# Splitting the summed weights one step earlier, and signalling the activation differences in two steps, in a fast-product feed-forward kernel

## The chip, the cores and the metric

One core of a Trainium2 chip runs the whole program. The metric is device time in microseconds (us) of one execution. Engines are named as the profile names them: PE is TensorE (its sequencer PEq), PEld its weight loads, DVE is VectorE, ACT is ScalarE, POOL is GpSimd, SP only issues transfers. Instructions of one engine run in program order; between engines there are only semaphores.

## The reference, cut to what matters

Two layers, each with two SwiGLU feed-forward sublayers ("FFN steps") around a mixer; all in float32, 640 tokens (512 sample, 128 prompt), model width 1024, inner width 2816:

```python
def _swiglu(h, wg, wu, wd):
    return (jax.nn.silu(h @ wg) * (h @ wu)) @ wd

def _layer(x, mod, p, tables, ctx_ckv, ctx_krope):
    ...
    h = _rmsnorm(x, p["norm_ffn1"]) * (1 + sc1) + sh1
    x = x + 0.5 * g1 * _swiglu(h, p["w_ffn1_gate"], p["w_ffn1_up"], p["w_ffn1_down"])
    ...
    x = x + g2 * m
    h = _rmsnorm(x, p["norm_ffn2"]) * (1 + sc3) + sh3
    x = x + 0.5 * g3 * _swiglu(h, p["w_ffn2_gate"], p["w_ffn2_up"], p["w_ffn2_down"])
    return x, ckv_n, krope
```

`mod` (the shifts sh, scales sc and gates g) comes from a small product of conditioning vectors with `w_mod`.

## The kernel before, in words

**Split products.** Every operand is held as a rounded part (`_hi`, made by ACT) and a remainder (`_lo`, made by DVE as whole minus rounded part, by the helper `lo_of`, L1830). A product is three matmuls: hi by hi (L731), hi weights by lo activations (L733), lo weights by hi activations (L735).

**Seven products for eight.** An FFN step has 22 pairs (one tile of 128 gate columns and one of 128 up columns). Gate and up, and the two halves of the model width, form a 2 by 2 block product, computed by seven products of half size, P1 to P7, each 4 tiles by 3 matmuls of 320 or 322 columns. They use sums of weight tiles, made by POOL in `weight_sums` in three additions (L695 for S1 and S3, L699 for S2, L702 for S4), and differences of activation halves. For pair g, weights are split in five pieces: `hi_11/lo_11` for P1, `hi_12/lo_12` for P2, `hi_22/lo_22` for P4, `hi_s/lo_s` (two summed tiles, 1024 columns) for P5 and P6, and `hi_34/lo_34` (the other two summed tiles, 1024 columns) for P3 and P7.

**The order of a cycle.** PE runs, for pair g: P2, P6, P5, P7, then P1 of pair g + 1, sometimes small products for `mod` (L785), then P4 and P3. PE waits for the `lo` piece of each. P3 of the pair g - 1 is thus the last product ahead of P2 of pair g. DVE combines the results from PSUM: `c11` (L2007), `u2` (L2012), `u2_p5` (L2018), `u3` (L2023), `c22` (L2028), `c21` (L2032), then the up half is scaled (`up_scaled`, L2038); `c12` (L2043) and `gate_scaled` (L2048) finish the gate of the pair one cycle later, `gated` (L2053) multiplies after ACT's `silu_of` (L1436) and `up_bias` (L1442), and `a_rest` makes `a_lo` after ACT's `a_part` (L1448). `ga` and `ub`, `prod` and `silu` are views of one buffer, so `c11` of a pair waits for `gated` of the one before.

**POOL.** The sums of pair g + 1 may start when both summed pieces of pair g are split (`s_los`, `s_lo34`), since `sums_raw` holds one pair. For the first pair of a chunk they wait for the down tiles instead.

**Chunks.** The 22 pairs are in four chunks of 5 or 6 (16 chunks in the program: eight of 6, eight of 5). After a chunk the eight down tiles are computed with `a_hi`, `a_lo` and added to `x` by DVE (L1969). For the first pair of a chunk the summed pieces are split during the down tiles.

**The start of an FFN step.** For k = 0 to 7, ACT scales a tile of x (`split_h`, L1411, L1414), DVE makes two steps of differences (L1844, L1833, L1850) and `h_lo`; after each odd k `split_differences(nn, i)` rounds three pieces on ACT (L1419 `t_hi` of 640 columns, L1420 `t_hi` and L1421 `h_hi` of 320) and takes three remainders on DVE (`t_lo` twice, `h_lo`). P6 of the first pair waits for each i (`s_tlo`). ACT's `copy_a1` (L1431), the first in a chain to `norm_rows` (L771: ACT `hi_11`, DVE `lo_11`, `c11`, `u2`, `lo_12`, `u2_p5`, `c12`, a reciprocal, ACT `diagonal` L1366), and POOL's sums of the second pair wait for all of them.

Of the kernel before, what the change touches and what calls it, by code (L numbers as in the profile page):

```python
# [267 lines left out]
def build(nc, i, o):  # L268
    ctx = ExitStack()
    with ctx:  # L270
# [386 lines left out]
        @block.gpsimd  # L657
        def _(pool):
            pool.sem_inc(s_split, CREDIT)
            pool.sem_inc(s_rot, START)  # L660
            nc.gpsimd.memset(ones[:], 1.0).then_inc(s_fill, 1)
            nc.gpsimd.memset(eps[:], EPS).then_inc(s_fill, 1)
            nc.gpsimd.memset(cond[:], 0.0).then_inc(s_fill, 1)
            nc.gpsimd.memset(ident[:], 0.0).then_inc(s_fill, 1)
            nc.gpsimd.memset(r_one[:, T:TB], 1.0).then_inc(s_fill, 1)
            pool.wait_ge(s_fill, 5)
            nc.gpsimd.affine_select(out=ident[:], in_=ident[:], compare_op=ALU.not_equal, fill=1.0, base=0,
                                    pattern=[[-1, P]], channel_multiplier=1).then_inc(s_fill, 1)
            nc.gpsimd.memset(group_ones[0][:, 0:1], 1.0).then_inc(s_fill, 1)

            def rotate(hd):

                pool.wait_ge(s_q32, hd + 1)
                nc.gpsimd.tensor_tensor(rot[NOPE:QK], q32[QK:P], rope_tab[QK:P, :], ALU.mult).then_inc(s_rot, 1)
                pool.wait_ge(s_rot, hd * 3 + 1 + START)
                nc.gpsimd.tensor_tensor(q32[NOPE:QK], q32[NOPE:QK], rope_tab[NOPE:QK, :], ALU.mult).then_inc(s_rot, 1)
                pool.wait_ge(s_rot, hd * 3 + 2 + START)
                nc.gpsimd.tensor_tensor(q32[NOPE:QK], q32[NOPE:QK], rot[NOPE:QK], ALU.add).then_inc(s_rot, 1)

            def weight_sums(pair):  # L680

                f, t = divmod(pair, PAIRS)
                w = raws[pair % 2]
                pool.wait_ge(s_pair[pair % 2], (pair // 2 + 1) * 16)
                if t == 1:
                    pool.wait_ge(s_tlo, (f + 1) * KT // 2)
                if fresh(pair):
                    if pair:
                        pool.wait_ge(s_split, (f // 2 + 1) * MIX_CHUNKS + CREDIT)
                elif chunk_of(pair)[1] and pair != 2 * PAIRS:  # L690
                    pool.wait_ge(s_dlo, tiles_before(pair))
                else:
                    pool.wait_ge(s_los, pair)
                    pool.wait_ge(s_lo34, pair)
                nc.gpsimd.tensor_tensor(sums_raw[:, UNIT:3 * UNIT].rearrange("p (s c) -> p s c", s=2),  # L695
                                        w.rearrange("p (s c) -> p s c", s=2)[:, :, 0:UNIT],
                                        w[:, 2 * UNIT:4 * UNIT].rearrange("p (s c) -> p s c", s=2), ALU.add).then_inc(s_s1, 1)
                pool.wait_ge(s_s1, pair + 1)
                nc.gpsimd.tensor_tensor(sums_raw[:, 3 * UNIT:4 * UNIT], sums_raw[:, 2 * UNIT:3 * UNIT], w[:, 0:UNIT],  # L699
                                        ALU.add).then_inc(s_s2, 1)  # L700
                pool.wait_ge(s_s2, pair + 1)
                nc.gpsimd.tensor_tensor(sums_raw[:, 0:UNIT], sums_raw[:, 3 * UNIT:4 * UNIT], w[:, UNIT:2 * UNIT],  # L702
                                        ALU.add).then_inc(s_s4, 1)

            for l in range(DEPTH):
                for pair in range(2 * l * PAIRS + (l > 0), (2 * l + 1) * PAIRS):
                    weight_sums(pair)
                pool.wait_ge(s_split, 2 * l * MIX_PAIRS + COS_C + 1 + CREDIT)
                rotate(l * HEADS)
                pool.wait_ge(s_rot, (l * HEADS + 1) * 3 + START)  # L710
                pool.wait_ge(s_out, (l + 1) * 32)
                pool.wait_ge(s_chunk, 2 * l * MIX_PAIRS + CHAN_C + 1 + CREDIT)
                for s in range(2):
                    nc.gpsimd.memset((v0, v1)[s][:, :, (1 - s) * VD:(2 - s) * VD], 1.0).then_inc(s_fill, 1)
                    pool.wait_ge(s_fill, 7 + 2 * l + s + 1)
                for h in range(1, HEADS):
                    rotate(l * HEADS + h)
                for pair in range((2 * l + 1) * PAIRS, (2 * l + 2) * PAIRS + (l + 1 < DEPTH)):
                    weight_sums(pair)
# [3 lines left out]
        def _(pe):  # L723
# [153 lines left out]
            def ffn_step(l, f, nn):  # L877
# [12 lines left out]
                def cycle(g, following, c, n):  # L890
# [8 lines left out]
                    else:  # L899
# [2 lines left out]
                    pe.wait_ge(s_los, g + 1)  # L902
                    pe.wait_ge(s_xupd, xupd0 + KT * c)
                    up_product(g, "P6", ext, unit(4), differences(t_hi, HALF, TB), differences(t_lo, HALF, TB),
                               (lambda i: pe.wait_ge(s_tlo, step * KT // 2 + i + 1)) if start else None)
                    up_product(g, "P5", HALF, unit(3), differences(t_hi, 0, HALF), differences(t_lo, 0, HALF))
                    if start:
                        norm_columns(nn)
                    pe.wait_ge(s_lo34, g + 1)
                    up_product(g, "P7", HALF, unit(6), first_half(h_hi, 0), first_half(h_lo, 0))  # L910
                    if following:
# [366 lines left out]
        def _(act):  # L1278
# [122 lines left out]
            def split_h(nn, k):  # L1401

                n = nn // 3 * 2 + nn % 3 // 2
                h32, from0 = (odd32, 0) if k % 2 else (even32, HALF)
                if k < 2:
                    act.wait_ge(s_tlo, n * KT // 2)
                else:
                    act.wait_ge(s_tsum, n * KT // 2 + k // 2)
                    act.wait_ge(s_hlo, nn * KT + k - 1 + START)
                for g, (v, to) in groups(x[:, ORDER[k], :], h32):  # L1410
                    ins = nc.scalar.activation(to, v, ACT.Copy, scale=scale_a[:, g, ORDER[k]:ORDER[k] + 1])  # L1411
                ins.then_inc(s_h32, 1)
                act.wait_ge(s_h32, n * KT + k + 1)
                nc.scalar.activation(h_hi[:, ORDER[k], from0:T], h32[:, from0:T], ACT.Copy).then_inc(s_hhi, 1)  # L1414

            def split_differences(nn, i):
                n = nn // 3 * 2 + nn % 3 // 2
                act.wait_ge(s_tsum, n * KT // 2 + i + 1)
                nc.scalar.activation(t_hi[:, i, 0:T], diff_n, ACT.Copy)  # L1419
                nc.scalar.activation(t_hi[:, i, TB:TB + HALF], diff_t[:, HALF:T], ACT.Copy)  # L1420
                nc.scalar.activation(h_hi[:, i, 0:HALF], diff_t[:, 0:HALF], ACT.Copy).then_inc(s_thi, 1)  # L1421
            def hi_part(k):
# [4 lines left out]
            def copy_a1(g):  # L1427
                act.wait_ge(s_product, DONE[g, "P1"])
                act.wait_ge(s_u2, g)
                act.wait_ge(s_tlo, (g // PAIRS + 1) * KT // 2)  # L1430
                nc.scalar.activation(p1_copy, bank(up_bank(g, "P1"), 0, TB - HALF), ACT.Copy).then_inc(s_a1, 1)  # L1431

            def silu_of(g):
# [16 lines left out]
            def ffn_step(l, f, nn):  # L1450
# [3 lines left out]
                def cycle(g, c, n):  # L1454
# [2 lines left out]
                    if following:  # L1457
                        hi_11(g + 1)
                    if not first:
                        hi_34(g)  # L1460
                        silu_of(g - 1)
                    if following:
                        hi_12(g + 1)
# [16 lines left out]
                    if last:  # L1480
                        hi_down(step, c, 1)
                    else:
                        hi_22(g + 1)
                    up_bias(g)

                for c in range(4):
# [306 lines left out]
        def _(dve):  # L1793
# [41 lines left out]
            def split_h(nn, k):  # L1835
# [4 lines left out]
                dve.wait_ge(s_h32, n * KT + k + 1)  # L1840
                if k % 2 == 0:
                    if n + i:
                        dve.wait_ge(s_tlo, n * KT // 2 + i)
                    tt(diff_n[:, 0:HALF], even32[:, HALF:T], even32[:, 0:HALF], ALU.subtract).then_inc(s_dn, 1)  # L1844
                else:
                    dve.wait_ge(s_dn, dn + 1)
                    minus_sum(diff_n[:, HALF:T], diff_n[:, 0:HALF], odd32[:, 0:HALF]).then_inc(s_dn, 1)
                    if k == KT - 1:
                        lo_h(nn, k)
                    tt(diff_t[:, 0:HALF], odd32[:, 0:HALF], even32[:, 0:HALF], ALU.subtract)  # L1850
                    dve.wait_ge(s_dn, dn + 2)
                    minus_sum(diff_t[:, HALF:T], diff_n[:, HALF:T], odd32[:, HALF:T]).then_inc(s_tsum, 1)
# [3 lines left out]
            def lo_h(nn, k):  # L1856
                h32, from0 = (odd32, 0) if k % 2 else (even32, HALF)
                dve.wait_ge(s_hhi, nn * KT + k + 1)
                lo_of(h_lo[:, ORDER[k], from0:T], h32[:, from0:T], h_hi[:, ORDER[k], from0:T]).then_inc(s_hlo, 1)

            def split_differences(nn, i):
                n = nn // 3 * 2 + nn % 3 // 2
                dve.wait_ge(s_thi, n * KT // 2 + i + 1)
                lo_of(t_lo[:, i, 0:T], diff_n, t_hi[:, i, 0:T])
                lo_of(t_lo[:, i, TB:TB + HALF], diff_t[:, HALF:T], t_hi[:, i, TB:TB + HALF])
                lo_of(h_lo[:, i, 0:HALF], diff_t[:, 0:HALF], h_hi[:, i, 0:HALF]).then_inc(s_tlo, 1)

# [193 lines left out]
            def ffn_step(l, f, nn):  # L2061
# [3 lines left out]
                def cycle(g, c, n):  # L2065
# [8 lines left out]
                    if following:  # L2074
                        lo_11(g + 1)
                    if not first:
                        lo_34(g)
                        gated(g - 1)
                    c11(g)
                    u2(g)  # L2080
# [17 lines left out]
                        lo_down(step, c, 1)  # L2098
                    else:
                        lo_22(g + 1)  # L2100
                    if first and c and vector_of(step, c - 1, 1):
                        mod_add(vector_of(step, c - 1, 1))
                    if n == KT // 2 and vector_of(step, c, 0):
# [403 lines left out]
```

## Time and profile before

| | |
|---|---|
| median of 3 runs | 2731.36 us (2730.28 to 2731.52) |
| profiled execution, its own time | 2732.1 us |
| its span | 2730.3 us |
| PE busy | 2662.0 us, 97% of the span |
| DVE busy | 2089.2 us, 77% |
| ACT busy | 1213.6 us, 44% |
| POOL busy | 625.4 us, 23% |

The span reaches from the first to the last instruction of the profiled execution; 1.8 us of its own time lie around it. PE counts as busy while a matmul is in flight, and consecutive matmuls overlap: a matmul of 320 columns shows 0.31 us, and the next one starts 0.15 us after it. In a timeline, a bracket at the end of a row tells how long the engine was idle ahead of it, and what ended that.

### The profile page before, as it was taken

How to read it: one execution, taken by the hardware profiler on the slowest of the kernel's cores; microseconds unless marked ns; L12 is line 12 of the kernel's file. 1: busy time of each engine (PE TensorE's matmuls, PEld its weight loads, DVE VectorE, ACT ScalarE, POOL GpSimd, SP SyncE). 2: the span in 40 equal slices, each digit the busy share in tenths (PEclk: the TensorE clock that was granted, in tenths of full speed). 3: DMA queues.
4: the chain of work that ended last, by engine and by line, in shares of the span. 5: the costliest groups of instructions: out<-in, count | busy, mean ns of one | idle time of the engine just before them, and what ended most of it. 6: DMA issues, size and time to landing. Idle time of an engine off the chain costs nothing. (4 is left out here: it accounts for less than half of the span.)

```text
span 2730.3 us, 44482 instructions
## 1 busy us (share of the span) xinstructions
PE 2662.0 (97%) x17686; PEld 2524.2 (92%) x17686; DVE 2089.2 (77%) x2832; ACT 1213.6 (44%) x2002; POOL 625.4 (23%) x327
## 2 busy tenths in 40 slices
PE   5999999999999999999999999999999999999997
PEld 3999999987899999999989999999779999999997
DVE  6978879766566788887988878887565668786876
ACT  5523435556422543343564334355563245343433
POOL 1322412023000124232321423300220003232230
PEclk9999999999999999999999999999999999999998
DMA  6434232210243243332234333322113322222312
GB/s 231 159 124 139 93 109 74 70 44 32 74 129 107 100 162 120 124 127 89 89 108 151 112 124 107 95 64 69 29 37 118 129 78 78 93 83 65 108 47 78
DMA packets 87694, 270.90 MB, mean 99 GB/s; under 512 B 8705, under 2 KB 12545, under 8 KB 87361
## 3 DMA queue, kind: packets, MB, share of 16 engines
q1 hardware_dynamic: 86048, 263.51, 29.3%
q10 hardware_dynamic: 1440, 4.56, 0.5%
q8 instruction: 141, 2.31, 0.3%
q14 instruction: 65, 0.52, 0.1%
HBM read 265.12 MB, written 2.92 MB: 98 GB/s over the span
## 5 line engine op out<-in xcount | busy, mean ns | idle before, releaser
L695 POOL TENSOR_TENSOR sums_raw<-raw_pairs 128x1024 f32<-128x1024 f32 x88 | 243.8, 2770 | 1613.7 <-DVE weights_lo L1830 1029.3
L731 PE MATMUL ps<-h_hi,weights_hi 128*128 128x322 f32 (+1 forms) x1408 | 440.3, 313 | 8.6 <-DVE t_lo L1830 3.1
L735 PE MATMUL ps<-h_hi,weights_lo 128*128 128x322 f32 (+1 forms) x1408 | 437.2, 311 | 0.0
L733 PE MATMUL ps<-h_lo,weights_hi 128*128 128x322 f32 (+1 forms) x1408 | 436.7, 310 | 0.0
L1830 DVE TENSOR_TENSOR weights_lo<-sums_raw,weights_hi 128x1024 fp32r<-128x1024 f32 (+2 forms) x296 | 329.5, 1114 | 65.2 <-ACT weights_hi L1341 28.2
L731 PE MATMUL ps<-t_hi,weights_hi 128*128 128x322 f32 (+1 forms) x1056 | 332.3, 315 | 5.3 <-DVE h_lo L1830 5.3
L735 PE MATMUL ps<-t_hi,weights_lo 128*128 128x322 f32 (+1 forms) x1056 | 327.5, 310 | 0.0
L733 PE MATMUL ps<-t_lo,weights_hi 128*128 128x322 f32 (+1 forms) x1056 | 326.5, 309 | 0.0
L731 PE MATMUL ps<-a_hi,weights_hi 128*128 128x320 f32 x1408 | 322.1, 309 | 3.6 <-DVE tmp L2032 3.3
L733 PE MATMUL ps<-a_lo,weights_hi 128*128 128x320 f32 x1408 | 320.8, 308 | 0.0
L735 PE MATMUL ps<-a_hi,weights_lo 128*128 128x320 f32 x1408 | 320.6, 309 | 0.0
L731 PEld LDWEIGHTS ps<-h_hi,weights_hi 128*128 128x128 f32 x1408 | 265.8, 189 | 16.7 <-issue 10.6
L1830 DVE TENSOR_TENSOR weights_lo<-raw_pairs,weights_hi 128x512 fp32r<-128x512 f32 x264 | 266.3, 1011 | 14.5 <-ACT weights_hi L1305 14.5
L733 PEld LDWEIGHTS ps<-h_lo,weights_hi 128*128 128x128 f32 x1408 | 266.2, 189 | 0.0
L735 PEld LDWEIGHTS ps<-h_hi,weights_lo 128*128 128x128 f32 x1408 | 266.1, 189 | 0.0
L731 PEld LDWEIGHTS ps<-a_hi,weights_hi 128*128 128x128 f32 x1408 | 234.5, 188 | 8.0 <-issue 3.8
L733 PEld LDWEIGHTS ps<-a_lo,weights_hi 128*128 128x128 f32 x1408 | 235.2, 188 | 0.0
L735 PEld LDWEIGHTS ps<-a_hi,weights_lo 128*128 128x128 f32 x1408 | 235.1, 188 | 0.0
L731 PEld LDWEIGHTS ps<-t_hi,weights_hi 128*128 128x128 f32 x1056 | 198.5, 188 | 17.8 <-issue 11.1
L1331 ACT ACTIVATE weights_hi<-sums_raw 128x1024 fp32r<-128x1024 f32 x88 | 93.2, 1060 | 269.8 <-POOL sums_raw L699 159.3
L1969 DVE SCALAR_TENSOR_TENSOR x<-ps,half_g,x 128x512 f32<-128x512 f32 (+1 forms) x256 | 128.7, 544 | 99.5 <-PE ps L735 99.4
L1352 ACT ACTIVATE weights_hi<-sums_raw 128x640 fp32r<-128x640 f32 (+1 forms) x120 | 94.4, 786 | 241.1 <-PE ps L735 217.4
(288 smaller groups left out, 5741.6 us busy)
## 6 DMA issues: line engine op xcount, KB each, us to landing
raw_pairs<-in_w_up SPq DMA_DIRECT2D x87, 1024.0 KB, 5.0
wm<-in_w_mod SPq DMA_DIRECT2D x72, 512.0 KB, 3.8
raw<-in_w_merge SPq DMA_DIRECT2D x32, 704.0 KB, 4.1
sums_raw<-in_w_down SPq DMA_DIRECT2D x56, 384.0 KB, 3.2
sums_raw<-in_w_down SPq DMA_DIRECT2D x64, 320.0 KB, 2.9
wm<-in_w_mod SPq DMA_DIRECT2D x48, 256.0 KB, 2.9
raw<-in_w_in SPq DMA_DIRECT2D x16, 512.0 KB, 3.6
late_wm<-in_w_mod SPq DMA_DIRECT2D x16, 512.0 KB, 3.6
```

The lines of the kernel that those rows point to most:

```text
L695: nc.gpsimd.tensor_tensor(sums_raw[:, UNIT:3 * UNIT].rearrange("p (s c) -> p s c", s=2), w.rearrange("p (s c) -> p s c", s=2)[:, :, 0:UNIT ...
L731: nc.tensor.matmul(out, whi, v, start=first, stop=False)
L733: nc.tensor.matmul(out, whi, v, start=False, stop=False)
L735: mm = nc.tensor.matmul(out, wlo, v, start=False, stop=last)
L1331: nc.scalar.activation(weights_hi[:, 3 * UNIT:5 * UNIT], sums_raw[:, 2 * UNIT:4 * UNIT], ACT.Copy).then_inc(s_his, 1)
L1352: nc.scalar.activation(weights_hi[:, w:w + n * P], down_raw(step, c, j), ACT.Copy).then_inc(s_dhi, 1)
L1830: return tt(out, whole, hi.bitcast(F32), ALU.subtract)
L1969: ins = stt(out=v, in0=y, scalar=gate[:, g, bass.ds(k + col, 1)], in1=v, op0=ALU.mult, op1=ALU.add)
```

## The change

It has two parts.

**Differences in two steps.** `split_differences` is cut in two. The first piece (`t_hi` of 640 columns on ACT, its `t_lo` on DVE) waits only for the first step of differences (`s_dn`) and has its own signal; the other two wait for the second step (`s_tsum`). So `s_thi` and `s_tlo` count twice per i, and all waits on them are renumbered. For the last i, DVE takes the first remainder ahead of the second step of differences. P6 of an FFN step's first pair waits for the first pieces alone, P7 then for all of them.

**Summed tiles earlier.** `hi_34(g)` on ACT moves from cycle g, behind `hi_11(g + 1)`, to the end of cycle g - 1, ahead of `up_bias(g - 1)`. `lo_34(g)` on DVE moves from cycle g, behind `lo_11(g + 1)`, to the end of cycle g - 1, behind `lo_22(g)`. It is so for 72 of 88 pairs; the other 16, the first of each chunk, stay as they were.

```diff
@@ weight_sums (POOL)
                 if t == 1:
-                    pool.wait_ge(s_tlo, (f + 1) * KT // 2)
+                    pool.wait_ge(s_tlo, (f + 1) * KT)
@@ cycle (PE)
-                               (lambda i: pe.wait_ge(s_tlo, step * KT // 2 + i + 1)) if start else None)
+                               (lambda i: pe.wait_ge(s_tlo, step * KT + 2 * i + 1)) if start else None)
...
                         norm_columns(nn)
+                        pe.wait_ge(s_tlo, (step + 1) * KT)
                     pe.wait_ge(s_lo34, g + 1)
@@ split_differences (ACT)
+                act.wait_ge(s_dn, n * KT + 2 * i + 2)
+                nc.scalar.activation(t_hi[:, i, 0:T], diff_n, ACT.Copy).then_inc(s_thi, 1)
                 act.wait_ge(s_tsum, n * KT // 2 + i + 1)
-                nc.scalar.activation(t_hi[:, i, 0:T], diff_n, ACT.Copy)
@@ copy_a1 (ACT)
-                act.wait_ge(s_tlo, (g // PAIRS + 1) * KT // 2)
+                act.wait_ge(s_tlo, (g // PAIRS + 1) * KT)
@@ ffn_step, cycle (ACT)
                     if not first:
-                        hi_34(g)
                         silu_of(g - 1)
...
                         hi_22(g + 1)
+                        hi_34(g + 1)
                     up_bias(g)
@@ split_h (DVE)
                     if k == KT - 1:
                         lo_h(nn, k)
+                        lo_normal(nn, i)
@@ split_differences (DVE)
+            def lo_normal(nn, i):
+                n = nn // 3 * 2 + nn % 3 // 2
+                dve.wait_ge(s_dn, n * KT + 2 * i + 2)
+                dve.wait_ge(s_thi, n * KT + 2 * i + 1)
+                lo_of(t_lo[:, i, 0:T], diff_n, t_hi[:, i, 0:T]).then_inc(s_tlo, 1)
...
-                dve.wait_ge(s_thi, n * KT // 2 + i + 1)
-                lo_of(t_lo[:, i, 0:T], diff_n, t_hi[:, i, 0:T])
+                if i < KT // 2 - 1:
+                    lo_normal(nn, i)
+                dve.wait_ge(s_thi, n * KT + 2 * i + 2)
@@ ffn_step, cycle (DVE)
                     if not first:
-                        lo_34(g)
                         gated(g - 1)
...
                         lo_22(g + 1)
+                        lo_34(g + 1)
```

The instructions of DVE from the end of one cycle into the next, in the first chunk, before (`up_scaled`, `lo_22`, `c12`, `gate_scaled`, `lo_11`, `lo_34`, `gated`, `c11`):

```order
L2038 TENSOR_TENSOR tmp<-tmp,r_one 128x642 [waits rstd_ready,up_second_half,up_first_half]
L1830 TENSOR_TENSOR weights_lo<-raw_pairs,weights_hi 128x512 [waits a22_hi]
L2043 TENSOR_TENSOR tmp<-ps,tmp 128x320 [waits sum_p1_p6_p5,products_done]
L2048 TENSOR_TENSOR tmp<-tmp,r_one 128x642 [waits gate_first_half,gate_second_half]
L1830 TENSOR_TENSOR weights_lo<-raw_pairs,weights_hi 128x512 [waits a11_hi]
L1830 TENSOR_TENSOR weights_lo<-sums_raw,weights_hi 128x1024 [waits s3_s4_hi]
L2053 TENSOR_TENSOR tmp<-tmp 128x640 [waits up_biased,silu_ready]
L2007 TENSOR_TENSOR tmp<-ps,tmp 128x322 [waits product_ready,p1_copied,products_done]
```

and the same place now (the lines lie 2 to 10 further down in the file):

```order
L2048 TENSOR_TENSOR tmp<-tmp,r_one 128x642 [waits rstd_ready,up_second_half,up_first_half]
L1832 TENSOR_TENSOR weights_lo<-raw_pairs,weights_hi 128x512 [waits a22_hi]
L1832 TENSOR_TENSOR weights_lo<-sums_raw,weights_hi 128x1024 [waits s3_s4_hi]
L2053 TENSOR_TENSOR tmp<-ps,tmp 128x320 [waits sum_p1_p6_p5,products_done]
L2058 TENSOR_TENSOR tmp<-tmp,r_one 128x642 [waits gate_first_half,gate_second_half]
L1832 TENSOR_TENSOR weights_lo<-raw_pairs,weights_hi 128x512 [waits a11_hi]
L2063 TENSOR_TENSOR tmp<-tmp 128x640 [waits up_biased,silu_ready]
L2017 TENSOR_TENSOR tmp<-ps,tmp 128x322 [waits product_ready,p1_copied,products_done]
```

`lo_34` (the row of 1024 columns that waits for `s3_s4_hi`) now stands ahead of `c12`, `gate_scaled` and `lo_11`, where it stood behind them.

ACT at the same place, before (`hi_22`, `up_bias` in two instructions, `hi_11`, `hi_34`, `silu_of` in two):

```order
L1319 ACTIVATE weights_hi<-raw_pairs 128x512 [waits products_done]
L1442 ACTIVATE tmp<-tmp 128x2x256 [waits up_scaled]
L1442 ACTIVATE tmp<-tmp 128x128
L1305 ACTIVATE weights_hi<-raw_pairs 128x512 [waits products_done,pair_loaded1]
L1341 ACTIVATE weights_hi<-sums_raw 128x1024 [waits products_done,sum_s4_ready]
L1436 ACTIVATE tmp<-tmp 128x2x256 [waits gate_scaled]
L1436 ACTIVATE tmp<-tmp 128x128
```

and now:

```order
L1320 ACTIVATE weights_hi<-raw_pairs 128x512 [waits products_done]
L1342 ACTIVATE weights_hi<-sums_raw 128x1024 [waits products_done,sum_s4_ready]
L1444 ACTIVATE tmp<-tmp 128x2x256 [waits up_scaled]
L1444 ACTIVATE tmp<-tmp 128x128
L1306 ACTIVATE weights_hi<-raw_pairs 128x512 [waits products_done,pair_loaded1]
L1438 ACTIVATE tmp<-tmp 128x2x256 [waits gate_scaled]
L1438 ACTIVATE tmp<-tmp 128x128
```

`hi_34`, which waits for P3 of the pair before, now stands ahead of `up_bias` and `hi_11`.

## Rows read from the trace of the kernel before

**Rows 1.** The page, busy time of PE.

```profile
PE 2662.0 (97%) x17686; PEld 2524.2 (92%) x17686; DVE 2089.2 (77%) x2832; ACT 1213.6 (44%) x2002; POOL 625.4 (23%) x327
```

**Rows 2.** Waits of PE: waiting for what, us in total, times, longest.

```profile
PE ps L731 <- DVE h_lo L1830: 5.8, 5, 1.5
...
PE ps L731 <- DVE tmp L2032: 3.3, 3, 2.2
```

**Rows 3.** Timeline of PE, one cycle: start, duration, line, operands.

```profile
202.95 0.31 PE L731 MATMUL ps<-h_hi,weights_hi 128*128 128x322 f32 x1
...
204.72 0.31 PE L731 MATMUL ps<-t_hi,weights_hi 128*128 128x322 f32 x1
...
210.05 0.31 PE L731 MATMUL ps<-h_hi,weights_hi 128*128 128x322 f32 x1
...
216.14 0.31 PE L731 MATMUL ps<-h_hi,weights_hi 128*128 128x322 f32 x1
```

**Rows 4.** Timeline of DVE, the same cycle.

```profile
202.71 0.69 DVE L1830 TENSOR_TENSOR weights_lo<-raw_pairs,weights_hi 128x512 fp32r<-128x512 f32 x1
203.31 0.48 DVE L2043 TENSOR_TENSOR tmp<-ps,tmp 128x320 f32<-128x320 f32 x1
203.90 0.83 DVE L2048 TENSOR_TENSOR tmp<-tmp,r_one 128x642 f32<-128x642 f32 x1
204.65 0.69 DVE L1830 TENSOR_TENSOR weights_lo<-raw_pairs,weights_hi 128x512 fp32r<-128x512 f32 x1
205.35 1.23 DVE L1830 TENSOR_TENSOR weights_lo<-sums_raw,weights_hi 128x1024 fp32r<-128x1024 f32 x1
206.50 0.82 DVE L2053 TENSOR_TENSOR tmp<-tmp 128x640 f32<-128x640 f32 x1
...
208.26 1.86 DVE L1830 TENSOR_TENSOR weights_lo<-raw_pairs,weights_hi 128x512 fp32r<-128x512 f32 x1
...
210.44 1.50 DVE L1830 TENSOR_TENSOR a_lo<-tmp,a_hi 128x640 fp32r<-128x640 f32 x1
...
212.79 1.39 DVE L1830 TENSOR_TENSOR weights_lo<-sums_raw,weights_hi 128x1024 fp32r<-128x1024 f32 x1
214.57 0.49 DVE L2032 TENSOR_TENSOR tmp<-ps,tmp 128x322 f32<-128x322 f32 x1 [0.40 <-PE ps L735]
...
215.90 0.69 DVE L1830 TENSOR_TENSOR weights_lo<-raw_pairs,weights_hi 128x512 fp32r<-128x512 f32 x1
```

**Rows 5.** Timeline of POOL, the same cycle.

```profile
206.75 2.82 POOL L695 TENSOR_TENSOR sums_raw<-raw_pairs 128x1024 f32<-128x1024 f32 x1 [6.80 <-DVE weights_lo L1830]
209.65 1.61 POOL L699 TENSOR_TENSOR sums_raw<-sums_raw,raw_pairs 128x512 f32<-128x512 f32 x1
211.34 1.75 POOL L702 TENSOR_TENSOR sums_raw<-sums_raw,raw_pairs 128x512 f32<-128x512 f32 x1
```

**Rows 6.** Timeline of ACT, the same cycle.

```profile
202.83 1.02 ACT L1442 ACTIVATE tmp<-tmp 128x512 f32<-128x512 f32 x2 [0.81 <-DVE tmp L2038]
...
204.28 1.04 ACT L1341 ACTIVATE weights_hi<-sums_raw 128x1024 fp32r<-128x1024 f32 x1
```

**Rows 7.** Timeline of POOL and DVE in the first chunk.

```profile
70.68 2.40 POOL L695 TENSOR_TENSOR sums_raw<-raw_pairs 128x1024 f32<-128x1024 f32 x1 [10.10 <-DVE weights_lo L1830]
...
71.61 2.15 DVE L2053 TENSOR_TENSOR tmp<-tmp 128x640 f32<-128x640 f32 x1 [1.10 <-ACT tmp L1436]
```

**Rows 8.** Timeline at the starts of the first and second FFN step.

```profile
43.63 0.61 PE L731 MATMUL ps<-h_hi,weights_hi 128*128 128x322 f32 x1 [3.07 <-DVE t_lo L1830]
...
53.01 1.23 DVE L1830 TENSOR_TENSOR t_lo<-tmp,t_hi 128x640 fp32r<-128x640 f32 x2 [1.53 <-ACT h_hi L1421]
...
940.61 0.41 PE L731 MATMUL ps<-t_hi,weights_hi 128*128 128x322 f32 x1 [1.13 <-DVE h_lo L1830]
...
948.09 1.34 PE L771 MATMUL ps<-tmp,ones 128*128 128x320 f32 x4 [0.37 <-ACT tmp L1366]
```

**Rows 9.** Windows: busy PE, PEld, DVE, ACT, POOL, granted PE clock, DMA share, GB/s.

```profile
1292.00:1360.00 68.00, 65.83 (x447) 65.61 (x447) 61.95 (x91) 36.67 (x63) 24.84 (x12) 1.00 0.31 101
```

More of the change, by code:

```diff
@@ L1405, in split_h @@
                 if k < 2:
-                    act.wait_ge(s_tlo, n * KT // 2)
+                    act.wait_ge(s_tlo, n * KT)
                 else:
@@ L1842, in split_h @@
                     if n + i:
-                        dve.wait_ge(s_tlo, n * KT // 2 + i)
+                        dve.wait_ge(s_tlo, n * KT + 2 * i)
                     tt(diff_n[:, 0:HALF], even32[:, HALF:T], even32[:, 0:HALF], ALU.subtract).then_inc(s_dn, 1)
```

## The prediction

> **What bounds it now.** The page first: PE is busy 97% of the span [rows 1], so time can be won only from PE's few waits, and lost by every new one. The list of PE's waits comes next. The one that the first part of the change aims at, PE behind `h_lo` of the difference tiles, is 5.8 us in all [rows 2]. No wait in that list is for P7's weights, which the second part prepares earlier, so that part has nothing to win directly. What it can lose is read from the timeline of a steady cycle. PE needs 1.77 us per product (P2 at 202.95, P6 at 204.72) and 13.19 us per cycle with its `mod` products [rows 3]; seven products alone are 12.40 us. DVE runs nearly without a stop in that cycle: `lo_22` starts at 202.71 and again at 215.90, and the only pause is 0.40 us [rows 4]. DVE is thus the engine that becomes the bound as soon as its cycle grows by more than that.
>
> **DVE and POOL collide.** `lo_12` takes 1.86 us instead of 0.69: it starts at 208.26 while POOL's first addition runs until 209.57, and ends 0.55 us after that; `a_rest` takes 1.50 instead of 0.82 and `lo_s` 1.39 instead of 1.23, behind POOL's second and third [rows 4, 5]. `gated` at 71.61 does the same: 2.15 us, ending 0.68 us after POOL's 70.68 + 2.40 [rows 7]. So a DVE instruction with both inputs in SBUF that starts under a POOL addition ends 0.55 (512 columns) or 0.69 us (640 columns) after that addition. The combining steps that read PSUM, which fill most of POOL's time now, are not held. Collisions cost DVE 1.17 + 0.68 + 0.16 = 2.0 us of this cycle; without them, the pause and 0.1 us of waiting for `hi_34`, its work is 13.19 - 2.0 - 0.4 - 0.1 = 10.7 us.
>
> **The second part, step by step.** `hi_34` now waits for P3 of the pair before, about 203.15 here, and takes 1.04 us [rows 6]; `lo_34` runs about 204.2 to 205.45, where PE wants it at 208.27: it has 1.7 us of slack already, so this gains nothing. `up_bias` goes from 202.83 to about 204.1 and is still hidden, as `silu_of` ends later. But POOL starts 0.17 us after `lo_34` ends (206.58, 206.75), and what stands behind `lo_34` on DVE is now `c12` and `gate_scaled`. Count from the end of `lo_34`:
> - `c12` reads PSUM and runs; `gate_scaled` could start at 0.51 (0.08 overlap, then 0.59 as from 203.31 to 203.90). POOL's first addition is in front, 0.17 to 2.57. It ends at 3.26; the next starts at 3.18 instead of 1.26: 1.9 us lost.
> - POOL's second addition follows until about 4.4 (0.08 between, 1.75 behind a held instruction of 640 columns). `lo_11` ends at 4.96 instead of 2.5 and loses 1.1 us more.
> - The third runs until about 6.1; `gated` ends at 6.8 and loses 1.1 us.
>
> That is 4.1 us in place of 2.0: a DVE cycle of 10.7 + 4.1 = 14.8 us against PE's 12.4 to 13.6. The later steps then find POOL idle, which is counted, and POOL can't fall out of this place, since its start is tied to `lo_34`. PE is held at P1 of the next pair, which wants `lo_11`: 210.24 or later in this cycle against 210.05 [rows 3], and a full cycle's difference from the next one on.
>
> **How many.** POOL starts behind `lo_34` in n - 2 cycles of a chunk of n: 56 in all. The first of each chunk costs about 0.4 us (12 times; in the first chunk of an FFN step `c12` isn't behind `lo_34` there, `gate_scaled` goes first, and nothing is lost, which also saves some 1 us later, 4 times). In the 40 others PE waits 14.8 less its own cycle: 20 without `mod` products 2.4, 12 with one `mod` vector's (13.19) 1.6, 8 with doubled ones (about 13.6) 1.2: 48 + 19 + 10 = 77 us. With 5 less 4 for the firsts: 78 us. At the end of a chunk DVE still lags: from the end of `lo_34` to the end of `c21` of the last pair it needs about 7.6 us with `gate_scaled`, 1.0 us of silu, `gated`, five combinations, `a_rest` and one down piece, and PE arrives after 0.95 + 3 x 1.77 = 6.3: 1.4 us in the eight chunks of 6, and with the last `a_lo` about the same in the chunks of 5: 22 us. Each restart of PE costs 0.1 us (a first matmul of 0.41 for 0.31, as at 940.61 [rows 8]): some 75 times, 7 us. Of the 3.3 us that PE waits for `c21` today [rows 2] some 1.5 are in these already. Second part: 78 + 22 + 7 - 1.5 = 105 us.
>
> **The first part.** At the second, third and fourth FFN start PE's wait at P6 (1.13 us at 940.61 [rows 8]) goes, because the first `t_lo` piece is there 3 us sooner. It isn't won: `norm_rows` at 948.09 already waits 0.37 us for a chain that begins with ACT's `copy_a1`, and this still waits for all pieces. Their end moves back rather than forward, since DVE now waits for ACT's rounding, which stands behind the square: about 0.17, 0.4 and 0.17 us. In the first FFN step DVE has pauses there, 1.53 us before the last `t_lo` [rows 8], and ACT's rounding moves into ACT's own pauses: about 0.9 us earlier at the first P1 (43.63), another 1.2 at the last pieces, 2.1 us in all. Together -2.1 + 0.75 = -1.3 us; the bounds are all of the 5.8 us won, and the 2.1 us not won.
>
> **Sum.** 105 - 1.3 = 104, rounded down to 102 for a few cycles at chunk edges. On the profiled execution's 2732.1 us that is 2834; the median of the runs is 0.7 us less, so 2833 us.
>
> **A rule weighed against a row.** A DVE instruction of 640 columns that was held ends 0.69 us after POOL's addition, and alone it takes 0.82 [rows 4, 5, 7]. The Trainium skill (SBUF — State Buffer, Who interferes with whom) says that whoever issues first gets the shared pair for the whole instruction and the other fully blocks. By that the held one would take its whole 0.82 us afterwards: 0.13 us more, three times in 56 cycles, and the sum would be 22 us higher. I go by the rows.
>
> **Rivals.**
> - **GpSimd comes second.** `gate_scaled` gets in ahead of POOL in every cycle, as `gated` does now (206.50 against 206.75). For it: the two are 0.34 us apart. Against: POOL's 0.17 us is short of 0.51. Then `lo_11` and `gated` are held, together 2.7 us: a DVE cycle of 13.4, 20 x 1.0 + 12 x 0.2 = 22 us, with the chunk ends about 33: 2764 us.
> - **DVE keeps up, and it gets faster.** The point is a DVE cycle of 12.4 us, so collisions below 1.7 us. Then only the first part is left, and P3 and P7 can never wait: from -1.3 to, where `norm_rows` follows as well, -5.8 us: 2730 to 2725.5. For it: `lo_34` no longer stands between `gate_scaled` and `gated`. Against: the 14.8 us above, and 0.40 us of pause as the whole reserve.
> - **The clock falls as well.** PE pauses of 1 to 2.4 us every 14 us could lower the granted clock. In the window with a 2.17 us wait it was 1.00, that is the upper level of 2.4 GHz [rows 9]. If each of the 40 longer waits were followed by 12 matmuls at twice 0.15 us, 70 us would be added: 2900. The Trainium skill (TensorE: Matmul & The Clock Gate, Part 1: The HAM clock gate) has an idle engine go back to 1.2 GHz; no row here shows it for waits as short as these.
>
> **Chances.** The forecast 0.80, own range 2795 to 2860 (collisions of 3.5 to 4.5 us per cycle, chunk ends 0 to 35 us); POOL second 0.08; DVE keeps up 0.09, split evenly between faster and the same; clock 0.03. About 0.2% (5.5 us) is what a measurement can tell from no change. Faster 0.04, same 0.05, slower 0.91. The range is 2785 to 2870; it leaves out the first two rivals and the third.
>
> **What would show it.** Right: PE's list of waits is led by L731 behind DVE's `weights_lo` (P1's), some 75 us; the line of `gate_scaled` (now L2058) has a mean well above its 0.83 us, near 2.7 in chunk middles, `lo_11` near 1.8 and `gated` near 1.9, while `lo_12` and `a_rest` are back at 0.69 and 0.82; cycle to cycle P2 starts 14.8 us apart; PE's wait at P6 is gone and the one at L771 is 1.2 us or more. Wrong: `gate_scaled` at 0.83 everywhere, P2 starts 12.4 apart, or a clock below 1.00 in the FFN windows.

## The result and the profile after

| | before | changed |
|---|---|---|
| median of 4 runs | 2731.44 us | 2843.19 us (2840.67 to 2845.33) |
| profiled execution, its own time | 2732.1 us | 2840.67 us |
| its span | 2730.3 us | 2838.7 us |

The changed kernel is slower by a factor of 1.0409, 95% interval 1.0396 to 1.0422: 111.8 us between the medians, where 102 were forecast. 2843 us lies in the range of 2785 to 2870.

The page of the changed kernel, busy times [rows 1]:

```profile
PE 2693.4 (95%) x17686; PEld 2540.1 (89%) x17686; DVE 2193.9 (77%) x2832; ACT 1218.4 (43%) x2002; POOL 603.0 (21%) x327
```

Every engine runs as many instructions as before, but DVE is busy 104.7 us longer (2089.2 before). The same work takes longer, so something holds it: the profile counts a held instruction as busy. DVE's share of the span (77%) is the same before and after and tells nothing of it.

PE's waits in the changed kernel (waiting for what, us in total, times, longest) [rows 2]:

```profile
PE ps L731 <- DVE weights_lo L1832: 59.7, 55, 2.0
PE ps L731 <- DVE tmp L2042: 21.0, 15, 3.9
PE ps L785 <- DMA wm_start<-in_w_mod: 20.9, 13, 14.6
PE ps L771 <- ACT tmp L1367: 9.8, 5, 2.4
PE ps L731 <- DVE a_lo L1832: 4.3, 8, 0.8
```

The first row is P1 behind `lo_11` (3.0 us before), the second the first down tile of a chunk behind `c21` (3.3 before), the fourth `norm_rows` (3.9 before), the last a down tile behind `a_lo` (0.3 before). The wait at P6 for the difference tiles, 5.8 us before, is gone. The wait for the first `mod` weights (L785) stands in both kernels (21.0 before).

DVE in one steady cycle of the changed kernel, timeline (start, duration, line, operands) [rows 4]:

```profile
207.60 0.68 DVE L1832 TENSOR_TENSOR weights_lo<-raw_pairs,weights_hi 128x512 fp32r<-128x512 f32 x1
208.20 1.22 DVE L1832 TENSOR_TENSOR weights_lo<-sums_raw,weights_hi 128x1024 fp32r<-128x1024 f32 x1
209.33 0.48 DVE L2053 TENSOR_TENSOR tmp<-ps,tmp 128x320 f32<-128x320 f32 x1
209.92 2.73 DVE L2058 TENSOR_TENSOR tmp<-tmp,r_one 128x642 f32<-128x642 f32 x1
212.58 1.77 DVE L1832 TENSOR_TENSOR weights_lo<-raw_pairs,weights_hi 128x512 fp32r<-128x512 f32 x1
214.27 1.91 DVE L2063 TENSOR_TENSOR tmp<-tmp 128x640 f32<-128x640 f32 x1
...
217.12 0.68 DVE L1832 TENSOR_TENSOR weights_lo<-raw_pairs,weights_hi 128x512 fp32r<-128x512 f32 x1
...
218.12 0.81 DVE L1832 TENSOR_TENSOR a_lo<-tmp,a_hi 128x640 fp32r<-128x640 f32 x1
...
222.23 0.69 DVE L1832 TENSOR_TENSOR weights_lo<-raw_pairs,weights_hi 128x512 fp32r<-128x512 f32 x1
```

POOL in the same stretch [rows 5], the bracket being its idle time before and what ended it:

```profile
209.59 2.39 POOL L695 TENSOR_TENSOR sums_raw<-raw_pairs 128x1024 f32<-128x1024 f32 x1 [8.72 <-DVE weights_lo L1832]
212.05 1.75 POOL L699 TENSOR_TENSOR sums_raw<-sums_raw,raw_pairs 128x512 f32<-128x512 f32 x1
213.88 1.61 POOL L702 TENSOR_TENSOR sums_raw<-sums_raw,raw_pairs 128x512 f32<-128x512 f32 x1
```

`lo_34` ends at 209.42 and POOL starts 0.17 us later, 0.33 us ahead of `gate_scaled`. That takes 2.73 us (0.83 alone) and ends 0.67 us after POOL's first addition; `lo_11` takes 1.77 (0.69) and ends 0.55 us after the second, `gated` 1.91 (0.82) and ends 0.69 us after the third. `lo_12` and `a_rest`, held before, are free. From `lo_22` to `lo_22` it is 14.63 us, and PE's P1 follows at the same pace, waiting each time:

```profile
214.41 0.41 PE L731 MATMUL ps<-h_hi,weights_hi 128*128 128x322 f32 x1 [1.19 <-DVE weights_lo L1832]
...
229.04 0.41 PE L731 MATMUL ps<-h_hi,weights_hi 128*128 128x322 f32 x1 [1.19 <-DVE weights_lo L1832]
```

### The profile page after: what moved, and what is told of

Same layout as the page of the kernel before. It is cut to its first block and busy times, and to the rows that moved or that the text cites. A ratio compares the mean times of both kernels' runs of the same rounds, so it can differ in the third digit from the quotient of the medians.

```text
span 2838.7 us, 44502 instructions
## 1 busy us (share of the span) xinstructions
PE 2693.4 (95%) x17686; PEld 2540.1 (89%) x17686; DVE 2193.9 (77%) x2832; ACT 1218.4 (43%) x2002; POOL 603.0 (21%) x327
## 5 line engine op out<-in xcount | busy, mean ns | idle before, releaser
L695 POOL TENSOR_TENSOR sums_raw<-raw_pairs 128x1024 f32<-128x1024 f32 x88 | 222.5, 2528 | 1729.2 <-DVE weights_lo L1832 1140.6
L731 PE MATMUL ps<-h_hi,weights_hi 128*128 128x322 f32 (+1 forms) x1408 | 447.3, 318 | 63.8 <-DVE weights_lo L1832 59.7
L1832 DVE TENSOR_TENSOR weights_lo<-sums_raw,weights_hi 128x1024 fp32r<-128x1024 f32 (+2 forms) x296 | 319.8, 1081 | 75.1 <-ACT weights_hi L1342 39.5
L733 PEld LDWEIGHTS ps<-t_lo,weights_hi 128*128 128x128 f32 x1056 | 201.2, 191 | 0.3
L735 PEld LDWEIGHTS ps<-t_hi,weights_lo 128*128 128x128 f32 x1056 | 200.7, 190 | 0.0
```

The source lines that it names most:

```text
L731: nc.tensor.matmul(out, whi, v, start=first, stop=False)
L733: nc.tensor.matmul(out, whi, v, start=False, stop=False)
L735: mm = nc.tensor.matmul(out, wlo, v, start=False, stop=last)
L1832: return tt(out, whole, hi.bitcast(F32), ALU.subtract)
```

## The experiments

All ratios are to the kernel before, run beside each version on the same chip. Its median there lay between 2730.8 and 2732.2 us. A ratio of 1.002 is 5.5 us.

### The two parts apart

The first part of the diff alone:

> The first part of the change alone; hi_34 and lo_34 where they stood. Theory: PE's wait at P6 goes (5.8 us), PE's wait at L771 grows from 3.9 to about 9.8 us as in the changed kernel, and the first P1 comes 1 us sooner: 2730 us, 1.3 less than before, ratio 0.9995. Rival (the wait at L771 of the changed kernel came from the second part): all 5.8 us are won, 2725.5 us, ratio 0.998.

Measured: 2734.0 us, ratio 1.0005 (0.9997 to 1.0014). No gain, perhaps a small loss. The trace says why: the wait at P6 is gone, and the one at L771 has grown as much (the list of PE's waits):

```profile
PE ps L771 <- ACT tmp L1367: 9.7, 5, 2.4
```

The rival falls. The growth at L771 belongs to the first part. The profiled execution (span 2730.4 us, against 2730.3 before) also has one dip of the granted clock more, worth some 1.7 us by the windows explained below; so the small loss isn't the first part's for certain.

The second part alone (`hi_34` and `lo_34` moved as in the diff):

> The second part alone; the difference tiles signalled as before. Theory: all of the loss is here, with the same cycle of 14.6 us, gate_scaled near 2.7 and lo_11 near 1.8 us in chunk middles, and the same dips of the granted clock after chunk ends: 2844 us, ratio 1.041 to 1.042. Rival (the two parts add to each other, through the pieces at an FFN step's start): under 1.035.

Measured: 2846.6 us, ratio 1.0414 (1.0400 to 1.0429). PE waits 58.6 us at P1, 54 times, with the same 1.95 us in the cycles without `mod` products as in the changed kernel. The whole loss is in this part.

### Without POOL's additions

In the second part alone, POOL adds one column instead of 512 or 1024, for all pairs but the first of each chunk. The sums of the weight tiles are thus left out, and the output is not that of the reference; only the time is of use.

```diff
-                nc.gpsimd.tensor_tensor(sums_raw[:, UNIT:3 * UNIT]..., w..., w[:, 2 * UNIT:4 * UNIT]..., ALU.add)
+                nc.gpsimd.tensor_tensor(sums_raw[:, UNIT:UNIT + 1], w[:, 0:1], w[:, 2 * UNIT:2 * UNIT + 1], ALU.add)
...
```

> The second part alone, with POOL's three additions cut to one column each for every pair but the first of a chunk (the sums of the weight tiles are left out there, all waits and signals stay). Theory (it is POOL's additions that hold DVE): DVE needs 10.7 us of work and 0.5 us of waiting for silu in a cycle, under PE's 12.4: no wait at P1, at most the three waits for c21 of before, 2725 to 2735 us. Rival (DVE's new order costs by itself, since gated now waits for silu, which lo_34 used to cover): PE keeps half or more of the 60 us of waits at P1 or at the ends of chunks, above 2770 us.

Measured: 2736.7 us, ratio 1.0022 (1.0012 to 1.0031). DVE at the same place, timeline:

```profile
205.96 0.83 DVE L2058 TENSOR_TENSOR tmp<-tmp,r_one 128x642 f32<-128x642 f32 x1
206.71 0.69 DVE L1840 TENSOR_TENSOR weights_lo<-raw_pairs,weights_hi 128x512 fp32r<-128x512 f32 x1
207.88 0.83 DVE L2063 TENSOR_TENSOR tmp<-tmp 128x640 f32<-128x640 f32 x1 [0.48 <-ACT tmp L1446]
```

With the same order on DVE and ACT, the same waits and signals, and POOL's work taken away, 0.22% is left of 4.14%. This run and the three that follow settle the cause. Sums that come sooner are no other explanation: in the changed kernel `lo_s` starts without a pause. What is left, 5.9 us against before, is a little more than expected, and no clean price of the order. PE's waits for `c21` (6.4 us, ten times, where before it was 3.3, three times) and for `a_lo` (2.3 us, 0.3 before) are 5.1 us longer, but its other waits are shorter by about as much. In the profiled execution, which is 7.6 us longer than that of the kernel before, the granted clock accounts for some 5 us: its dips cost 10.3 us, against 5.1. The kernel before without POOL's additions was not run.

### POOL's start moved

The second part alone, with one wait more in `weight_sums`, for pairs that are not the first of a chunk:

```diff
                     pool.wait_ge(s_los, pair)
                     pool.wait_ge(s_lo34, pair)
+                    if not chunk_of(pair)[1]:
+                        pool.wait_ge(s_lo11, pair + 1)
```

> The second part alone, but POOL's sums of the next pair wait for lo_11 as well, so that they start while gated runs, as before the change; DVE's and ACT's order stay changed. Theory (the collisions with POOL make the cycle long): gate_scaled is back at 0.82, lo_11 at 0.69 and gated at 0.82 us, lo_12 and a_rest are held instead; a DVE cycle of 12.8 to 13.1 us, PE waits 0.3 to 0.7 us in 20 cycles and hardly at the ends of chunks, and the granted clock stays at 1.00: 2738 to 2752 us. Rival (lo_34 ahead of gate_scaled and lo_11 on DVE is itself what holds PE, by its 1.2 us per cycle): 56 times 1.2, above 2795 us.

Measured: 2806.3 us, ratio 1.0271 (1.0257 to 1.0285). **A miss**: faster than without the wait, but far from 2752. With `s_gsc, pair - 1` in its place:

> As the run before, but POOL's sums wait only for gate_scaled, so that they start under lo_11. Theory: gate_scaled and lo_11 take 0.82 and 0.69 us, gated is held by the first addition (1.9 us lost), lo_12 and a_rest by the second and third (0.3 and 0.7): a DVE cycle of 13.6 us, PE waits 1.2 us in 20 cycles and 0.4 in 12, with the ends of chunks 30 to 50 us: 2762 to 2782 us, between the run before and the changed kernel. Rival (DVE's order is what counts): the same as the run before, whichever that is.

Measured: 2787.1 us, ratio 1.0201 (1.0186 to 1.0217). **A miss** as well: 5 us above the expected range, and faster than POOL behind `lo_11`, where it was expected to be slower. The rival, that the two are the same, falls too. DVE and POOL with POOL behind `lo_11`:

```profile
225.40 0.69 DVE L1832 TENSOR_TENSOR weights_lo<-raw_pairs,weights_hi 128x512 fp32r<-128x512 f32 x1
226.57 2.77 DVE L2055 TENSOR_TENSOR tmp<-tmp 128x640 f32<-128x640 f32 x1 [0.48 <-ACT tmp L1438]
```

```profile
226.25 2.41 POOL L697 TENSOR_TENSOR sums_raw<-raw_pairs 128x1024 f32<-128x1024 f32 x1 [7.90 <-DVE weights_lo L1832]
```

`gated` was meant to be under way when POOL starts. But since `lo_34` no longer stands ahead of it, it waits 0.48 us for silu, which takes ACT 1.02 us after `gate_scaled` and which `lo_34` used to cover. POOL gets in 0.32 us ahead and `gated` takes 2.77 us (2.47 with POOL behind `gate_scaled`). With the wait put on `s_prod, pair - 1`, POOL cannot do so:

> The second part alone, POOL's sums waiting for gated of the pair before. In the run with POOL behind lo_11 the miss came from gated: without lo_34 ahead of it, it waits 0.5 us for silu, POOL gets in first and gated takes 2.8 us. Theory (that is the whole miss): gated is back at 0.82 us, lo_12 is held to 0.55 us behind the first addition (1.8 us lost), a_rest by the second (0.9), a DVE cycle of 13.5 us, as with POOL behind gate_scaled: 2778 to 2796 us, below the 2806 of POOL behind lo_11. Rival (the miss has another cause, in DVE's order): 2806 us or more.

Measured: 2787.5 us, ratio 1.0203 (1.0186 to 1.0220), inside the range. `gated` is back at 0.83 us, and the next two take the hold:

```profile
223.37 0.83 DVE L2055 TENSOR_TENSOR tmp<-tmp 128x640 f32<-128x640 f32 x1 [0.48 <-ACT tmp L1438]
...
225.14 2.17 DVE L1832 TENSOR_TENSOR weights_lo<-raw_pairs,weights_hi 128x512 fp32r<-128x512 f32 x1
...
227.63 1.50 DVE L1832 TENSOR_TENSOR a_lo<-tmp,a_hi 128x640 fp32r<-128x640 f32 x1
```

The cycle is 14.6 us with the second part alone, 13.85 with POOL behind `lo_11`, 13.55 behind `gate_scaled`, 13.49 behind `gated` (DVE, `lo_22` to `lo_22`). The time goes with it: 2847, 2806, 2787 and 2788 us. So with one order on DVE, the place at which POOL comes in sets the time. In these three runs the waits also show elsewhere: in steady cycles PE no longer waits at P1, but at P6 for `lo_s`, and most of all at the ends of chunks, here with POOL behind `gated`:

```profile
PE ps L733 <- DVE tmp L2034: 29.4, 16, 5.9
PE ps L733 <- DVE weights_lo L1832: 12.8, 16, 0.9
```

That is what the first two expectations had too low. For POOL behind `lo_11` the ends of chunks were to cost hardly anything, and the waits for `c21` are 34.7 us, 31 more than before; its steady cycle was too long as well, 13.85 us for 12.8 to 13.1, because of `gated`. For POOL behind `gate_scaled` the cycle was right (13.55 for 13.6), and the ends were given at most some 20 us, where the waits for `c21` grew by 27. That DVE's lag, too small to stop PE at P1, falls due at the end of a chunk is the likely reading; no run tests it. Dips of the clock have a part here too: 18.8, 12.0 and 13.7 us in the three profiled executions, 5.1 before.

### ACT's share

The kernel before with only `hi_34(g + 1)` behind `hi_22(g + 1)` on ACT, `lo_34` where it stood:

> Only ACT's share of the second part: hi_34 ahead of up_bias, lo_34 on DVE where it stood. Theory: hi_11 comes 1.0 us later, DVE has lo_34 no longer in front of lo_11 and waits for it, about 1.1 us per cycle, so DVE's cycle grows from 12.8 to about 13.9 us and PE waits in 20 to 32 cycles: 2765 to 2800 us. Rival (the later up_bias and hi_11 are hidden): 2732 us, ratio 1.000.

Measured: 2736.2 us, ratio 1.0020 (1.0011 to 1.0029). **A miss.** DVE does wait for `hi_11`, but 0.49 us and not 1.1:

```profile
218.21 0.69 DVE L1830 TENSOR_TENSOR weights_lo<-raw_pairs,weights_hi 128x512 fp32r<-128x512 f32 x1 [0.49 <-ACT weights_hi L1305]
```

That is about what DVE had in hand (its pause of 0.40 us in [rows 4]). The profiled execution, span 2733.2 us, shows only 1 us more of waits for `c21`, 4.3 against 3.3; the rest of the 0.2% isn't placed. The rival is nearer, though 1.000 lies outside the interval too, and DVE's reserve is seen to be small but real. ACT's share of the move alone thus costs about a twentieth of the 4.1%.

### The start of an FFN step

The first part alone, and on ACT:

```diff
@@ ffn_step, cycle (ACT)
                     if following:
                         hi_11(g + 1)
+                    if g == g0:
+                        copy_a1(g)
@@ ffn_step, chunks (ACT)
-                    copy_a1(g0 + tiles[0])
+                    if c:
+                        copy_a1(g0 + tiles[0])
```

> The first part alone, and at an FFN step's start ACT rounds hi_11 of the second pair ahead of copy_a1, so that this no longer waits for the last difference tiles. Theory (norm_rows is held by a chain in which lo_11 starts 1.1 us late and then runs under POOL's first addition for 1.96 us): lo_11 ends 2.4 us sooner, lo_12 is then held for 1 us more, the chain ends 1.5 us sooner, and PE's wait at L771 falls from 9.7 to about 4.5 us: ratio 0.998 against before, about 2727 us. Rival (another link holds the chain, the square root or P3): under 1 us, ratio 1.000.

Measured: 2728.3 us, ratio 0.9989 (0.9980 to 0.9998); the wait at L771 is 5.7 us, where 4.5 was expected. The direction is the theory's, but the gain is 0.11% where 0.2% was expected. Then POOL's first sums out of the way as well:

```diff
@@ weight_sums (POOL), second pair of an FFN step
                     pool.wait_ge(s_tlo, (f + 1) * KT)
+                    pool.wait_ge(s_lo12, pair + 1)
```

> As the run before, and POOL's sums of an FFN step's second pair wait for its lo_12, so that neither lo_11 nor lo_12 is held. Theory: another 1 us sooner at each of four starts, the wait at L771 at most 2.5 us (it is 2.2 at the program's end alone): ratio 0.9975, about 2725 us. Rival (POOL's later sums hold the second pair instead): a new wait at P6 of the second pair, 1.00 or more.

Measured: 2723.5 us, ratio 0.9968 (0.9956 to 0.9981), **faster than both kernels**. DVE with the first part alone, where `lo_11` waits for ACT and then lies under POOL's first addition:

```profile
938.11 0.49 DVE L1832 TENSOR_TENSOR h_lo<-tmp,h_hi 128x320 fp32r<-128x320 f32 x1
939.70 1.96 DVE L1832 TENSOR_TENSOR weights_lo<-raw_pairs,weights_hi 128x512 fp32r<-128x512 f32 x1 [1.11 <-ACT weights_hi L1306]
```

and with all three edits, where it follows at once and runs free:

```profile
936.75 0.49 DVE L1836 TENSOR_TENSOR h_lo<-tmp,h_hi 128x320 fp32r<-128x320 f32 x1
937.15 0.69 DVE L1836 TENSOR_TENSOR weights_lo<-raw_pairs,weights_hi 128x512 fp32r<-128x512 f32 x1
```

From the end of `h_lo` to the end of `lo_11` it is 3.06 us in the one and 0.60 in the other, and PE's list of waits now has

```profile
PE ps L772 <- ACT tmp L1368: 2.7, 2, 2.2
```

of which 2.2 us are the one at the program's end. PE's wait at P1 and P6 for weights is 3.0 us in three waits, as before, so the rival's new wait at P6 didn't come. Does the first part of the change have a share in this gain? The two edits without it, and beside that all three again:

> The two edits of the fastest run (hi_11 ahead of copy_a1, POOL's sums of the second pair behind lo_12) on the kernel before, without the first part of the change. Theory (the first part takes the wait at P6 away, and the two edits let it be kept): here the 5.8 us at P6 stay and only the wait at L771 falls, from 3.9 to 2.2 us: ratio 0.9994, about 2729.5 us. Rival (the two edits alone make the gain, the first part is worth nothing): ratio 0.997, as in the run with all three.

> The fastest version again, beside the run without the first part and against the same runs of the kernel before: ratio 0.996 to 0.998. If it comes out within 0.001 of the run without the first part, the first part is worth nothing.

Measured: 2727.2 us, ratio 0.9984 (0.9975 to 0.9993), and 2724.8 us, ratio 0.9971 (0.9961 to 0.9982). The two edits alone are worth more than the 0.9994 expected. The wait at L771 is 2.2 us as expected and the one at P6 stays (6.1 us); the rest of the gain isn't placed. The first part adds some 2.5 us. The two intervals against the kernel before overlap, but of the eleven executions without the first part nine are longer than every one of the seven with it, so its share is real, if small. Whether it would be 2.5 us again, no run tells.

## Why the prediction was right, step by step

**Right in its mechanism.** Each sign that was named for it came: the wait at P1 leads the list, with 59.7 us for the forecast 75; `gate_scaled` near 2.7, `lo_11` near 1.8 and `gated` near 1.9 us (measured 2.73, 1.77, 1.91); `lo_12` and `a_rest` back at 0.68 and 0.81; the wait at P6 gone and L771 grown. The run without POOL's additions and the three that move POOL's start show that the collisions are the cause, and not merely beside it. One sign that was named for being wrong came as well, a clock below 1.00 in the FFN windows; it is taken up below.

**The cycle of 14.8 us** was 14.63. The three holds cost 1.90, 1.08 and 1.09 us, together 4.07 where 4.1 was forecast. The rest of DVE's cycle, forecast at 10.7 us, was 14.63 - 4.07 = 10.56. The Trainium skill (SBUF — State Buffer, Who interferes with whom) has the other engine fully blocked until the first is through; here the held instructions ended 0.67, 0.55 and 0.69 us after POOL, each 0.13 to 0.16 us short of its own length alone, so by the rule the cycle would have been some 0.4 us longer than it was. The prediction was right to go by its rows. The same section of the Trainium skill says that an instruction of DVE with at most one input in SBUF, outside the 2-port modes, is not held; the trace agrees: in the kernel before, `u2_p5`, which reads PSUM, starts at 210.04 under POOL's second addition (209.65 to 211.26 [rows 5]) and takes 0.48 us, as it does without one (217.72 in the changed kernel).

**Steady waits, forecast 78 us and part of 7 for restarts.** The waits at P1 are 59.7 us against 3.0 before, so 56.7 more, 21 less than forecast. There are 17 of 1.95 us, 12 of 1.19, 7 of 0.8 (two of these, at the second pair of an FFN step, stand in the kernel before as well) and 19 of 0.45 or less (twelve are the firsts of chunks, 0.34 each). Where 1.95, 1.19 and 0.8 us were measured, 2.4, 1.6 and 1.2 were forecast. Of the 0.4 us, 0.17 is DVE's shorter cycle. The rest went to the restart of PE after a wait, which was forecast at 0.1 us, and is read from four starts: the first matmul of P2, that of P1 with the one behind it, and that of the next P2.

```profile
1335.41 0.31 PE L731 MATMUL ps<-h_hi,weights_hi 128*128 128x322 f32 x1
...
1344.61 0.41 PE L731 MATMUL ps<-h_hi,weights_hi 128*128 128x322 f32 x1 [1.95 <-DVE weights_lo L1832]
1344.86 0.31 PE L733 MATMUL ps<-h_lo,weights_hi 128*128 128x322 f32 x1
...
1350.03 0.31 PE L731 MATMUL ps<-h_hi,weights_hi 128*128 128x322 f32 x1
```

From P2 to P1 it is 9.20 us, and 7.10 in a cycle of the kernel before without a wait (411.20 to 418.30): the wait and 0.15 more, since the last matmul ahead of the wait has nothing to overlap with. From P1 to P2 it is 5.42 and was 5.30 (to 423.60), since the second matmul comes 0.25 us after the first and not 0.15. So a restart costs about 0.26 us, and PE's own cycle is 12.7 us with it and not 12.4. Three of the twenty plain cycles are missing for a reason of their own, below.

**Ends of chunks, forecast 22 us.** The waits for `c21` and `a_lo` grew by 17.7 + 4.0 us, close to the forecast; with 19 restarts more it is 27 us. The 1.4 us at the end of a chunk of six was 1.8 to 1.9 in six of the eight (the other two: 3.9, where it was 2.2 before, and 0.7), because DVE needs 8.2 us from the end of `lo_34` to the end of `c21` and not 7.6:

```profile
358.51 1.22 DVE L1832 TENSOR_TENSOR weights_lo<-sums_raw,weights_hi 128x1024 fp32r<-128x1024 f32 x1
...
362.15 0.83 DVE L2063 TENSOR_TENSOR tmp<-tmp 128x640 f32<-128x640 f32 x1 [0.48 <-ACT tmp L1438]
...
363.92 0.68 DVE L1832 TENSOR_TENSOR weights_lo<-raw_pairs,weights_hi 128x512 fp32r<-128x512 f32 x1
364.52 0.48 DVE L2028 TENSOR_TENSOR tmp<-ps,tmp 128x320 f32<-128x320 f32 x1
...
367.44 0.48 DVE L2042 TENSOR_TENSOR tmp<-ps,tmp 128x322 f32<-128x322 f32 x1
```

The wait of `gated` for silu was in the forecast. `lo_12` (363.92), which takes up 0.60 us of this stretch, doesn't stand in the prediction's list for it, and that is the difference. In the chunks of five the waits were 9.8 us where 11 were forecast, so the sum came out right.

**The first part, forecast -1.3 us.** It came out at +1.4 (ratio 1.0005, interval -0.8 to +3.8 us), so -1.3 is just outside and the sign isn't settled; the dip of the clock that its profiled execution has more, 1.7 us, would be more than half of the 2.7 us between the two, but one execution decides nothing. That the gain at P6 would go to `norm_rows` was right, 5.8 us away and 5.9 us back. What the prediction did not see is that two edits shorten the chain at each start, by 2.5 us from the end of `h_lo` to the end of `lo_11`.

**The third rival, the clock,** had a chance of 0.03 at 2900 us. The time did not go there, but the mechanism is in the trace. The changed kernel's windows (from and to, width, PE busy and its matmuls, granted clock, DMA share, GB/s):

```profile
446.00:450.00 4.00, 2.05 (x14) 1.00 0.55 225
450.00:454.00 4.00, 4.00 (x18) 0.57 0.00 0
454.00:458.00 4.00, 4.00 (x29) 1.00 0.01 4
```

After P1's wait of 1.95 us, which ends at 449.82, the granted clock is 0.57 as a mean over these 4 us: for most of them it is 0.5, the level of 1.2 GHz. It costs 0.43 x 4 = 1.7 us. Between 50 and 2710 us there are twelve such dips, against three before, 15 us more by the windows' sum of (1 - clock), 20.4 against 5.1. Not all of it is paid. DVE is the slower engine in a steady cycle, so PE's lost time comes off its next wait, 0.41 us where its like has 1.95:

```profile
449.82 0.41 PE L731 MATMUL ps<-h_hi,weights_hi 128*128 128x322 f32 x1 [1.95 <-DVE weights_lo L1832]
...
464.45 0.41 PE L731 MATMUL ps<-h_hi,weights_hi 128*128 128x322 f32 x1 [0.41 <-DVE weights_lo L1832]
```

The other two waits of this kind end at 2422.71 and 2639.15. These are the missing plain cycles, so the count of 20 and 12 was sound. Of the 8 cycles with doubled `mod` products five have the long wait of 0.8 us; the other three are the first of their chunk that lose anything, and have 0.33.

**The sum of the profiled executions,** 108.5 us: waits that changed 78 us (+56.7 at P1, +17.7 and +4.0 at the ends of chunks, +5.9 at L771, -5.8 and -0.3 for the difference tiles), 66 restarts more of 0.26 us 17 us, clock 15 us. That makes 110, and PE's other waits are 1 us shorter: nearly all is placed. The forecast of 102 against 111.8 was right in the mechanism, and the size is in part luck. Three terms were off and nearly cancel: the waits at P1 were 21 us too dear, the restarts 10 us too cheap, and the clock, 15 us, was in the sum at nothing.

## What to carry to other kernels

When an instruction that releases GpSimd is moved, price not only what waits for it but what stands behind it on VectorE for as long as GpSimd then works: in these traces the instructions with both inputs in SBUF were held (0.83 us became 2.73), those that read PSUM were not (0.48 us either way). In this kernel, where VectorE has 0.4 us in hand in a cycle, the order in which the two meet was worth 4%, and `lo_34`, which seemed to stand in a bad place, covered an activation there. The 5.8 us removed at P6 came back at L771; something was won only when the chain behind it was shortened too.

## What was not expected of the hardware

**A dip of the clock isn't tied to a place.** At the same end of a chunk with the same wait, 1.87 us at 368.18 in the changed kernel and 1.88 at 372.12 with the second part alone, the granted clock of the next 4 us is

```profile
368.00:372.00 4.00, 3.82 (x16) 0.57 0.61 185
```

in the one and

```profile
372.00:376.00 4.00, 3.88 (x26) 1.00 0.63 185
```

in the other. Both kernels have such dips at twelve places. The Trainium skill (TensorE: Matmul & The Clock Gate, Part 1: The HAM clock gate) has an idle engine go back to 1.2 GHz; here the same wait of under 2 us was followed by a fall in the one run and not in the other, and what decides was not tried.

**POOL pays too.** Its second addition, of 512 columns, takes 1.75 us in the changed kernel, where it alternates with held DVE instructions, and with VectorE idle, in the run with all three edits,

```profile
942.08 1.28 POOL L700 TENSOR_TENSOR sums_raw<-sums_raw,raw_pairs 128x512 f32<-128x512 f32 x1
```

1.28 us.
